# Transposed router logits, written-out expert passes and a new order of first loads in a four-layer two-stream transformer kernel

## The reference, cut to what matters

```python
def expert_choice_ffn(h, w_router, w_g, w_u, w_d):
    cap = CAPACITY_FACTOR * n // N_EXPERTS            # 32 of 256 tokens
    logits = jnp.einsum('bnd,de->ben', h, w_router)   # 16 experts
    aff = jax.nn.softmax(logits, axis=1)
    gate, idx = lax.top_k(aff, cap)
    xs = h[bi, idx]
    y = (silu(xs @ w_g) * (xs @ w_u)) @ w_d           # per expert, hidden width 1024
    return zeros.at[bi, idx].add(y * gate)
```

## Time and profile before

| | us |
|---|---|
| median of 3 runs | 2911.82 (2910.58 to 2915.54) |
| the profiled execution's own time | 2912.62 |
| its span, first to last instruction | 2910.4 |
| PE busy | 2645.1 (91%) |
| DVE busy | 974.1 (33%) |
| ACT busy | 563.5 (19%) |
| weights read | 336 chunks of 2 MB |

### The profile page before, as it was taken

The page is one execution under the profiler, slowest core; times in us unless marked ns, Lnnn a source line. Parts: engine busy times, 40 slices in busy tenths (PEclk is TensorE's granted clock), DMA queues, the critical chain, the costliest instruction groups (busy, mean ns, idle before and its releaser), DMA issues.

```text
span 2910.4 us, 28396 instructions
## 1 busy us (share of the span) xinstructions
PE 2645.1 (91%) x11372; PEld 1642.7 (56%) x11372; DVE 974.1 (33%) x2065; ACT 563.5 (19%) x1225; POOL 2.9 (0%) x8
## 2 busy tenths in 40 slices
PE   5999999999999999999997997988899997888787
PEld 4688888768887744544444342432377884233232
DVE  6612550541573244454633110110254333011010
ACT  2311120321212154310002011111354001000000
POOL 0000000000000000000000000000000000000000
PEclk9999999999999999999997999999999998999999
DMA  9614664623654310133432799999612746999998
GB/s 368 272 58 173 231 243 165 262 83 154 244 234 180 124 42 29 58 144 145 173 159 101 331 428 428 429 429 428 297 59 87 289 175 254 428 429 429 429 427 358
DMA packets 51517, 711.25 MB, mean 244 GB/s; under 512 B 5523, under 2 KB 7843, under 8 KB 8405
## 3 DMA queue, kind: packets, MB, share of 16 engines
q1 hardware_dynamic: 50902, 708.00, 59.3%
q0 software_dynamic: 512, 1.79, 0.2%
HBM read 708.72 MB, written 1.05 MB: 244 GB/s over the span
## 4 chain that ended last, share of the span: by engine, by line
PE 70%; DMA 22%; DVE 4%; ACT 3%; issue 2%; SPq 0%; ACTq 0%; DVEq 0%; PEldq 0%
PE bank L590 69%; DMA ring<-weights 22%; PE bank L589 1%; DVE ring L1372 1%; ACT work L1244 0%; ACT work L1252 0%; DVE X L1417 0%; DVE work L1398 0%; DVE work L1397 0%; DVE h L1408 0%; ACT work L1304 0%; DVE small L1595 0%; DMA cst<-const 0%; ACT work L1220 0%; ACT work L1219 0%
## 5 line engine op out<-in xcount | busy, mean ns | idle before, releaser
L590 PE MATMUL bank<-h,ring 128*128 128x256 f32 (+1 forms) x3840 | 1020.9, 426 | 31.3 <-ACT h L1113 29.0
L590 PEld LDWEIGHTS bank<-h,ring 128*128 128x128 f32 x3840 | 733.0, 192 | 305.1 <-issue 218.9
L590 PE MATMUL bank<-ring,work 128*64 128x512 f32 x3072 | 691.7, 598 | 136.7 <-DMA ring<-weights 130.1
L590 PEld LDWEIGHTS bank<-ring,work 128*64 128x64 f32 x3072 | 215.2, 137 | 586.9 <-issue 422.2
L590 PE MATMUL bank<-work,ring 128*128 128x256 f32 (+1 forms) x1728 | 456.4, 421 | 7.7 <-DVE X L1417 6.3
L590 PEld LDWEIGHTS bank<-work,ring 128*128 128x128 f32 x1728 | 328.8, 191 | 119.9 <-issue 83.1
L1723 DVE TENSOR_TENSOR work<-bank,work 128x512 f32<-128x512 f32 x32 | 22.1, 691 | 649.4 <-ACT work L1294 649.4
L1372 DVE SCALAR_TENSOR_TENSOR ring<-ring,crow 128x1024 f32<-128x1024 f32 x192 | 228.7, 1219 | 22.1 <-DMA ring<-weights 21.8
L590 PE MATMUL bank<-work 128*64 128x256 f32 (+4 forms) x1216 | 209.2, 383 | 26.6 <-ACT work L1244 10.3
L590 PEld LDWEIGHTS bank<-work 128*128 128x128 f32 (+2 forms) x1216 | 139.4, 180 | 88.2 <-issue 36.2
L1417 DVE SCALAR_TENSOR_TENSOR X<-bank,mod,X 128x256 f32<-128x256 f32 x152 | 67.9, 481 | 255.2 <-PE bank L590 254.6
(11 more groups left out here) (162 smaller groups left out, 1240.9 us busy)
## 6 DMA issues: line engine op xcount, KB each, us to landing
ring<-weights SPq DMA_DIRECT2D x336, 2048.0 KB, 19.7
X<-x_cols SPq DMA_DIRECT2D x1, 1024.0 KB, 18.0
X<-x_cols POOLq DMA_DIRECT2D x1, 1024.0 KB, 17.4
out<-X SPq DMA_DIRECT2D x2, 512.0 KB, 3.0
cst<-const SPq DMA_DIRECT2D x1, 914.5 KB, 4.8
cst<-const POOLq DMA_DIRECT2D x1, 512.0 KB, 23.5
pars<-par SPq DMA_DIRECT2D x1, 275.0 KB
work<-positions POOLq DMA_DIRECT2D x1, 128.0 KB, 7.7
```

Source lines behind the costliest of these rows:

```text
L590: nc.tensor.matmul(o, l, r, start=start, stop=stop)
```

## The change

1. **Logits.** The router matrix (16 columns) is the stationary side and h moves, nt columns per product; each of the eight products waits for its own tile of h only. The logits then lie experts by tokens. DVE copies them to SBUF (`lgc`), PE transposes them back (`lgt`), and DVE's maximum and subtraction read PSUM. Two banks of token transposes stand before `lgt`, two behind it, the rest behind the affinities; ACT's evictions are in the same order.
2. **Slots.** The fourth round has no match_replace. `eachrow` is made per stream, one operation and one signal each (in layer 1 only the first).
3. **Experts.** All four groups are written out on all engines; no loop is left but SP's. The gathers for group 0 (`x0`) move from `d0`/`d1` into the group: four first, then gate/up of chunk 0, two gathers, chunk 1, two gathers, chunks 2 and 3. Each gate/up part waits for the evictions of its two tiles.
4. **Start.** SP: c rows, chunks 0 to 3, x, chunk 4, constants, chunk 5. POOL: parameters, `vrow`, positions. A row of ones set by DVE (`one1`) takes the place of the constant in the `row` products, and PE waits for the constants after them. DVE does rows 0 and 1, the tiles of chunk 0, rows 2 and 3, chunk 1, rows 4 and 5, chunks 2 and 3. The angles come in `b0`, behind the tiles of own chunk 7 and before the latent means; their sines on ACT behind the last `ksb` eviction, and the sign product on DVE behind `z`. `csig` and `craw` lie elsewhere in SBUF.

```diff
-PHASES = ["a0", "b0", "b1", "d0", "e0", "y0", "d1", "e1", "y1"]
-TRIPS = {ph: GROUPS - 1 if ph[0] == "e" else 1 for ph in PHASES}
+PASSES = [[f"e{layer}{g}" for g in range(GROUPS)] for layer in range(2)]
+PHASES = ["a0", "b0", "b1", "d0"] + PASSES[0] + ["d1"] + PASSES[1]
...
-        out += [("logit", 0)] + [("afft", 0)] + each("htok", 4 if layer else 8)
-        out += [("cols", 0)] + each("bc", 1 if layer else 2) + each("xs", KT)
+        turns = each("htok", 4 if layer else 8)
+        out += [("logit", 0)] + turns[:2] + [("lgt", 0)] + turns[2:4] + [("afft", 0)] + turns[4:]
+        out += [("cols", 0)] + each("bc", 1 if layer else 2)
...
+        g = int(phase[2])
+        out = each("x0", 4) if g == 0 else []
+        out += [("eg", 0), ("eu", 0)]
+        out += each("x0", KT)[4:] if g == 0 else []
...
-            sp_.dma_start(cst[:, 0:NC_FIRST], const[:, 0:NC_FIRST]).then_inc(const_in, 16)
             for s in range(SLOTS):
+                if s == 4:
+                    sp_.dma_start(X[:, :, 0:T], x_cols[:, 0]).then_inc(x_in, 16)
                 sp_.dma_start(ring[:, s, :], weights[s]).then_inc(R.slot_full[s], 16)
-                if s == 1:
-                    sp_.dma_start(X[:, :, 0:T], x_cols[:, 0]).then_inc(x_in, 16)
-                    sp_.dma_start(pars1[:, :, :], par1[:, :, 0:N1]).then_inc(par_in, 16)
-                    sp_.dma_start(vrow[:, :, :], par1[0:1, :, N1:N1 + 512]).then_inc(par_in, 16)
+                if s == 4:
+                    sp_.dma_start(cst[:, 0:NC_FIRST], const[:, 0:NC_FIRST]).then_inc(const_in, 16)
...
+            pool.dma_start(pars1[:, :, :], par1[:, :, 0:N1]).then_inc(par_in, 16)
+            pool.dma_start(vrow[:, :, :], par1[0:1, :, N1:N1 + 512]).then_inc(par_in, 16)
...
-                pe.wait_ge(*h_ready.take(KT * nt // T))
-                bank = R.bank("logit")
-                product("logit", 0, [(bank[:, 16 * i:16 * i + 16], [(h[:, k, i * P:(i + 1) * P], ring[:, c % SLOTS, 16 * k:16 * k + 16])
-                                                                    for k in range(KT)]) for i in range(nt // P)])
+                pe.wait_ge(*R.free("logit"))
+                for k in range(KT):
+                    pe.wait_ge(*h_ready.take(nt // T))
+                    mm(R.bank("logit")[0:16, 0:nt], ring[:, c % SLOTS, 16 * k:16 * k + 16], h[:, k, 0:nt], k == 0, k == KT - 1,
+                       R.filled("logit") if k == KT - 1 else None)
                 used.append(c)
+
+                def to_tokens(i):
+                    tok, half = divmod(i, 2)
+                    turned("htok", i, [(R.bank("htok", i)[:, j * P:(j + 1) * P], h[:, 4 * half + j, tok * P:(tok + 1) * P])
+                                       for j in range(4)])
+
+                to_tokens(0)
+                to_tokens(1)
+                pe.wait_ge(*logits_copied.take())
+                turned("lgt", 0, [(R.bank("lgt")[:, 16 * i:16 * i + 16], lgc[0:16, i * P:(i + 1) * P]) for i in range(nt // P)])
+                to_tokens(2)
+                to_tokens(3)
                 pe.wait_ge(*affinities_ready.take())
                 turned("afft", 0, [(R.bank("afft")[0:32, i * P:(i + 1) * P], aff[:, i]) for i in range(2)])
-                for i in range(2 * nt // P):
-                    tok, half = divmod(i, 2)
-                    bank = R.bank("htok", i)
-                    turned("htok", i, [(bank[:, j * P:(j + 1) * P], h[:, 4 * half + j, tok * P:(tok + 1) * P]) for j in range(4)])
+                for i in range(4, 2 * nt // P):
+                    to_tokens(i)
                 pe.wait_ge(*slots_ready.take())
                 turned("cols", 0, [(R.bank("cols")[0:64, 0:32], seli[0:32, :])])
-                pe.wait_ge(*rows_ready.take())
                 for s in range(nt // T):
+                    pe.wait_ge(*rows_ready.take())
                     product("bc", s, [(R.bank("bc", s)[:, :], [(ones[0:32, :], eachrow[0:32, 16 * s:16 * s + 16].rearrange("p e r -> p (e r)"))])])
                 pe.wait_ge(*R.evac("htok", 2 * nt // P - 1))
                 pe.wait_ge(*R.evac("bc", nt // T - 1))
-                for d in range(KT):
-                    gather(d, nt, 0)
-
-                pe.wait_ge(*R.evac("xs", KT - 1))
...
+                if g == 0:
+                    for d in range(4):
+                        gather("x0", d, nt, 0)
+                for i in range(4):
+                    if g == 0:
+                        pe.wait_ge(*R.evac("x0", 2 * i + 1))
+                    gate_up(0, range(i, i + 1))
+                    if g == 0 and i < 2:
+                        gather("x0", 4 + 2 * i, nt, 0)
+                        gather("x0", 5 + 2 * i, nt, 0)
...
-            pe.wait_ge(const_in, 16)
             pe.wait_ge(c_in, 16)
+            pe.wait_ge(*one_ready.take())
             R.phase("a0")
             for j in range(6):
-                product("row", j, [(R.bank("row", j)[:, :], [(ones[0:1, :], craw[:, 512 * j:512 * j + 512])])])
+                product("row", j, [(R.bank("row", j)[:, :], [(one1[:, :], craw[:, 512 * j:512 * j + 512])])])
+            pe.wait_ge(const_in, 16)
...
-                with pe.Fori(0, GROUPS - 1) as g:
-                    book.enter(f"e{layer}", g)
-                    R.phase(f"e{layer}", g)
+                for g in range(GROUPS):
+                    R.phase(PASSES[layer][g])
                     experts(layer, g)
-                    book.leave(f"e{layer}", GROUPS - 1)
-                R.phase(f"y{layer}")
-                experts(layer, GROUPS - 1, True)
...
+                if L == 0:
+                    for n in range(2):
+
+                        act.wait_ge(*angle_ready.take())
+                        A(trig[:, n], ang[:, 1 + n], ACT.Sin).then_inc(*angles_done.inc())
+                    logs_and_exps()
...
+            def angles():
+                dve.wait_ge(pos_in, 16)
...
+                    TS(a, a, 3.1415925, -3.1415925, ALU.min, ALU.max).then_inc(*angle_ready.inc())
...
-                flat = lg[:, 0:n].rearrange("p a e -> p (a e)")
-                nc.vector.tensor_copy(flat, R.bank("logit")[:, 0:16 * n]).then_inc(*R.freed("logit"))
-                dve.wait_ge(*R.evac("logit"))
-                settle(nc.vector.tensor_reduce(small[:, 0:n], lg[:, 0:n], AX, ALU.max))
-                TT(lg[:, 0:n], lg[:, 0:n], small[:, 0:n].unsqueeze(2).to_broadcast([P, n, 16]), ALU.subtract)\
+                nc.vector.tensor_copy(lgc[0:16, 0:nt], R.bank("logit")[0:16, 0:nt]).then_inc(*logits_copied.inc())
+                dve.wait_ge(*logits_copied.take())
+                dve.sem_inc(*R.freed("logit"))
+                dve.wait_ge(*R.full("lgt"))
+                tokens = R.bank("lgt")[:, 0:16 * n].rearrange("p (a e) -> p a e", e=16)
+                settle(nc.vector.tensor_reduce(small[:, 0:n], tokens, AX, ALU.max))
+                TT(lg[:, 0:n], tokens, small[:, 0:n].unsqueeze(2).to_broadcast([P, n, 16]), ALU.subtract)\
                     .then_inc(*logits_ready.inc())
                 dve.wait_ge(*logits_ready.take())
+                dve.sem_inc(*R.freed("lgt"))
...
-                    nc.vector.max_index(eidx[0:32, 8 * r:8 * r + 8], best, wk[0:32, :])
-                    settle(nc.vector.match_replace(wk[0:32, :], best, wk[0:32, :], -1.0))
+                    ins = nc.vector.max_index(eidx[0:32, 8 * r:8 * r + 8], best, wk[0:32, :])
+                    if r < 3:
+                        ins = nc.vector.match_replace(wk[0:32, :], best, wk[0:32, :], -1.0)
+                    settle(ins)
                 settle_to(nc.vector.tensor_copy(seli[0:32, 0:32], eidx[0:32, :]), slots_ready)
-                TT(eachrow[0:32], seli[0:32, 0:32].unsqueeze(1).to_broadcast([32, 32, CAP]),
-                   const_of("mine")[0:32].unsqueeze(2).to_broadcast([32, 32, CAP]), ALU.mult).then_inc(*rows_ready.inc())
+                for s in range(nt // T):
+                    es = slice(16 * s, 16 * s + 16)
+                    TT(eachrow[0:32, es], seli[0:32, 0:32].unsqueeze(1).to_broadcast([32, 16, CAP]),
+                       const_of("mine")[0:32, es].unsqueeze(2).to_broadcast([32, 16, CAP]), ALU.mult).then_inc(*rows_ready.inc())
...
-                gathered(nt)
...
+            rows((0, 1))
+            modulate(shares("a0", "")[:4], spent)
+            rows((2, 3))
+            modulate(shares("a0", "")[4:8], spent)
+            rows((4, 5))
+            modulate(shares("a0", "")[8:], spent)
             dve.wait_ge(par_in, 32)
             dve.wait_ge(x_in, 16)
+            dve.wait_ge(const_in, 16)
```

187 lines of the change are left out of this document (88 added, 99 removed).

## The result

| | before | after |
|---|---|---|
| median of 5 runs, us | 2913.97 (2910.58 to 2915.54) | 2897.47 (2892.22 to 2898.76) |
| the profiled execution | 2912.62 | 2898.13 |
| its span | 2910.4 | 2896.3 |
| PE busy | 2645.1 | 2641.4 |
| packets of q8 in the span | 75 (1.23 MB) | 90 (1.47 MB) |

The ratio of after to before is 0.9938 (95%: 0.9926 to 0.9950), 16.5 us at the medians. 2892.3 was forecast, with a range of 2885 to 2901. The sum, though, was made against the profiled execution, and there it is 14.1 us of span where 19.5 were forecast, and one term of 6.6 us in those 14.1 was not in the prediction at all.

A forecast was written before the change was run, and what follows sets the result against it. Bound: serial work ahead of each expert stage's first slot release; at the start, DMA and DVE. 0 + 13.1 + 7.0 - 0.6 = 19.5 us off the profiled 2912.62 gave 2893.1, less 0.8 to the median: 2892.3, range 2885 to 2901.

The forecast's parts named there:

- What bounds it: Expert stages: each ends a fixed time after the first slot release, so serial work ahead of that sets the time.
- The logits, layer 0: Layer 0's router: products of 512 columns behind each tile of h let DVE's maximum start 8.9 us sooner.
- rival A: Router logits: the clock does not rise, they take 14.1 and 7.0 us; 2899.7 us in all; chance 0.12.
- Rival C: First gathers: early release is not worth it, 7.4 us are missing; 2899.7 us in all; chance 0.08.
- Rival B: Start: it gains too, as const lands early and chunk 7 follows the stream; 3 us more, 2889.3; chance 0.17.
- Rival D: Written-out passes: code fetches through busy DMA engines stop PE; slower, 2918 at 6 us each; chance 0.03.
- Start: 0: Start up to z: no gain, z ending at 97.1 us as before; bounds -3 to +3 us gained.
- Layer 0: 13.1: Layer 0's router and first gathers: first slot release at 1601.3 instead of 1614.4, 13.1 us gained.
- Layer 1: 7.0: Layer 1's router and first gathers: first slot release at 2445.1 instead of 2452.1, 7.0 us gained.
- First gather 2437.8: Layer 1's router: the first gather starts at 2437.8 us, where it was 2441.96.
- and 3.5: Layer 1's first gate/up chunk: takes 3.5 us behind four gathers of 3.8, giving release at 2445.1.
- Written-out passes: -0.6: Expert passes: instructions fetched four times instead of two cost 0.3 us of stream per layer, -0.6 in all.

The follow-up runs named there:

- experiment 5: Changed kernel with all eight x0 gathers of a layer ahead of the first gate/up product; median 2898.97 us, ratio 0.9956.
- experiment 7: Changed kernel with useless products keeping PE busy in the idle time of the router phases; median 2894.23 us, ratio 0.9930.
- experiment 10: Changed kernel with earlier angles, empty bank turns ahead of the waits, and useless PE products, one fewer per layer behind the broadcasts; median 2885.39 us, ratio 0.9907.
- experiment 1: Changed kernel with the old bank order back, the `ssx` bank taken after four `down` banks; median 2904.00 us, ratio 0.9965.
- experiment 2: Kernel before with only the new bank order, the `ssx` bank taken ahead of the `down` banks; median 2906.89 us, ratio 0.9977.
- experiment 9: Changed kernel with the angles moved between own chunks 5 and 6 instead of behind own chunk 7; median 2891.76 us, ratio 0.9931.
- experiment 3: Kernel before with its expert groups written out instead of looped, no other edit; median 2916.81 us, ratio 1.0011.
- experiment 6: Changed kernel with PE's empty bank turns handled before the wait for the last broadcast's eviction, not after; median 2893.68 us, ratio 0.9943.
- experiment 4: Changed kernel with 2560 already fulfilled waits added on POOL, so that an idle engine fetches more code; one run, 2896.39 us.
- experiment 8: Changed kernel with the old logit product by tokens and DVE's old copy; one run, 2917.41 us.

## Why the prediction was right, and where it was not

**Confirmed.** What bounds it: in layer 0 the marks follow the first product (experiments 5, 7 and 10), and no hole opened in the rate. The logits, layer 0: 8.7 us at the maximum against 8.9; the clock rose within them (9.54 us, between the 7.0 of eight tiles at 0.88 and the 14.1 of eight at 1.76), so rival A did not come. The broadcasts met a cold PE as priced (3.78 us for two). Rival C (early release worth nothing) is refuted in layer 0: from the first gather to the mark it takes 99.25 us after and 103.12 before, 3.9 of the forecast 4.6, and experiment 5 puts 2.2 of them down to the order of the gathers. In layer 1 it is 102.77 against 103.37 in these two profiles, and not refuted. Rival B fell: const waited in SP's queue, and z came later, not sooner. Rival D, slower by fetches, has the direction of what the passes did and not its size, 3.2 us and not 25; that fetches do it is not shown.

**The step that was not there.** The list of edits had no bank order. The prediction went through the diff by its four headings, and a line of the plan was read as part of none. It brought 6.6 us of the 14.1 (experiments 1 and 2). Without it the kernel would have gained some 7.5 us of span, and 2904.0 at the median, outside the range of 2885 to 2901. That the forecast held the time is owed to this as much as to its own terms.

**Start: 0; it was -1.1 in this profile, -0.5 by the means.** When const lands was taken from the volume ahead of it (12.9 MB at the rate of before, 34.8 us). It landed at 36.2: SP, which stood at chunk 4, did not even issue it before 20.68. The sum has a slip of 0.2 besides, since 41.2 and 3.4 make 44.6 and not 44.8. And own chunk 7 landed at 70.47 instead of 69.1, with the products, angles and means behind it (81.56 for 80.3). Within the bounds of -3 to +3. Experiment 9 shows what the place of the angles cost at z: 1.6 to 2.2. If the loss of clock below belongs to the start, the start cost 3.7 to 4.3 us and lies outside its bounds.

**Layer 0: 13.1; it was 12.1 to 13.9.** Right in size. Within it, logits 0.2 less, two holes of 0.7 where 0.7 was counted for both, and slower gathers (5.62 us for four where 5.2 were taken). The 1.85 us called a loop entry were mostly empty turns, as experiment 3 shows; they left the path all the same. And the sum stood on a lucky profile of before: its two broadcasts took 1.98 us and its eight gathers 8.71, but 3.42 and 10.08 in experiment 2, with the same code there and the mark 1.8 us later.

**Layer 1: 7.0; it was 2.5 in this profile, 3.7 by the means.** This is the largest error among the terms, unless the clock's loss belongs to the start. The maximum came 2.7 us sooner, not 3.2 (the logits' clock rose later), and DVE's part was as drawn. Then two steps failed: "First gather 2437.8", because the seven empty turns on PE, 2.1 us, were not counted, although the plan gives them as plainly as the banks; and "and 3.5", because the first chunk was priced from a PE that had eight gathers behind it: the four gathers took 3.75 as forecast, but the chunk behind them still met the lower clock, 4.88. The end of the first chunk stood 34.71 + 3.47 = 38.18 us from the sum of squares and stands 29.82 + 4.88 = 34.70: 3.5 gained. Experiments 6 and 7 bring back 1.8 and 2.5 of the mark, both 4.3.

**Written-out passes: -0.6; they cost 3.2.** The step was "instructions are fetched four times where two copies were: 0.3 us of stream per layer". The bytes were right (q8 has 15 packets where it had 8), but not what the written-out code costs: experiment 3 has the 3.2 us without any other edit. Whether it is the fetching at all is open, since the fetches of experiment 4 fell outside the passes.

**The clock in `b0`: not foreseen**, 3.2 us, in after and in experiments 1, 4, 5, 7 and 8, and in none of before, 2, 3, 6, 9 and 10, with the same work there in all. It goes with the start: seven of the twelve profiles have the new start with the angles behind own chunk 7, and six of these seven have the drop. The five others, with the old start or the early angles, have none. In the seven PE idles 2.9 to 3.3 us for ACT ahead of its product at 102.7 to 105.2 us, in the five 1.2 to 1.3, and everything from there to the drop at some 145 us takes the same time. Experiment 6 has the long idle time (2.88) and keeps its clock, and no run changes this idle time alone, so that the one brings the other is suggested and not shown. Added back, the change is worth 17.3 us of span; but if the new start is what costs the 3.2, they are its price, which experiments 9 and 10 no longer pay.

## What to carry to other kernels

Read the diff by its lines and not by its purposes: what stands next to what in a rotation of banks is an edit, and costs what the latest reader of the reused bank costs. Where a stage is bound by the first release of a stream, count every instruction between the last wait and that release, waits and signals of empty turns too, and take the durations from rows of a PE that has idled as long. Written-out code cost 3 us where the loop stood beside a saturated stream. And before an experiment is read, look in its trace whether the edit took effect at its place: the fetches of experiment 4 came in another stage.
